# Four RWKV norm items moved between the output tiles of a hybrid encoder layer

## What is computed

```
h = rms_norm(x) ; u = h @ w_in                 # combined projection
y_a = rwkv7(u)   # 8 heads x 64, both directions; then per head a norm over 64,
                 #   y * lnx_w + lnx_b, + bonus, * g
y_b = hgrn2(u)   # 4 heads x 128, both directions; then per head
                 #   o * rsqrt(mean(o^2)) * gnorm_w, * silu(gate)
x = x + concat(y_a, y_b) @ w_out
h2 = rms_norm(x)
x = x + hierarchical_moe(h2)   # top-1 of 4 groups, top-2 of 8 experts in it, 32 experts
return rms_norm(x)
```

## Time and profile before

| | |
|---|---|
| median of 3 runs | 2428.27 us (2427.3 to 2428.68) |
| the profiled execution | 2425.25 us, span 2423.6 us |
| TensorE busy | 2266.9 us, 94% of the span |
| VectorE busy | 1028.8 us, 42% |
| ScalarE busy | 719.3 us, 30% |
| GpSimd busy | 418.3 us, 17% |
| DMA, mean | 180 GB/s, 436.48 MB |

### The profile page before, as it was taken

The page is one execution under the profiler, slowest core; times in us unless marked ns, Lnnn a source line. Parts: engine busy times, 40 slices in busy tenths (PEclk is TensorE's granted clock), DMA queues, the critical chain, the costliest instruction groups (busy, mean ns, idle before and its releaser), DMA issues. The chain is left out here.

```text
span 2423.6 us, 64805 instructions
## 1 busy us (share of the span) xinstructions
PE 2266.9 (94%) x28110; PEld 1485.1 (61%) x28110; DVE 1028.8 (42%) x2175; ACT 719.3 (30%) x1446; POOL 418.3 (17%) x520
## 2 busy tenths in 40 slices
PE   7989999989999999999968888995899999999997
PEld 4444544445555555555556656753788888888883
DVE  3236777634745645645645645543111111111115
ACT  4224554534544534534512312221000000000003
POOL 1002222200000000000012100012433334333331
PEclk9999999999999999999969988997899999999999
DMA  4113343533342432432366733251899999999986
GB/s 137 35 49 130 133 153 122 190 71 90 90 125 65 117 99 69 121 95 68 109 193 179 214 111 102 92 184 48 325 360 358 332 360 332 357 331 357 363 308 227
DMA packets 359836, 436.48 MB, mean 180 GB/s; under 512 B 164896, under 2 KB 296112, under 8 KB 351408
## 3 DMA queue, kind: packets, MB, share of 16 engines
q1 hardware_dynamic: 343232, 397.94, 48.2%
q0 software_dynamic: 14256, 35.04, 5.9%
q10 hardware_dynamic: 2112, 0.01, 0.1%
HBM read 329.87 MB, written 102.93 MB: 179 GB/s over the span
## 5 line engine op out<-in xcount | busy, mean ns | idle before, releaser
L1161 PE MATMUL h_pp<-hT,r_wcol 128*128 128x512 f32 x832 | 414.1, 621 | 9.1 <-ACT h_iraw L1289 9.1
L2715 PE MATMUL e_ps_gu<-e_xT,e_wg 128*128 128x128 f32 x2048 | 236.6, 277 | 18.3 <-DVE e_xT L2790 18.3
L2715 PEld LDWEIGHTS e_ps_gu<-e_xT,e_wg 128*128 128x128 f32 x2048 | 233.8, 194 | 18.8 <-DVE e_xT L2790 18.8
L2715 PEld LDWEIGHTS e_ps_gu<-e_xT,e_wu 128*128 128x128 f32 x2048 | 233.7, 192 | 14.8 <-issue 14.8
L2715 PE MATMUL e_ps_gu<-e_xT,e_wu 128*128 128x128 f32 x2048 | 233.9, 275 | 0.0
L2724 PE MATMUL e_ps_y<-e_wd,e_hid 128*128 128x512 f32 x512 | 225.1, 593 | 1.1 <-DVE e_hid L2804 1.1
L1161 PEld LDWEIGHTS h_pp<-hT,r_wcol 128*128 128x128 f32 x832 | 142.1, 190 | 130.2 <-issue 109.2
L500 PE MATMUL h_pp<-hT,r_wcol 128*128 128x512 f32 x480 | 209.0, 593 | 1.3 <-DVE hT L770 1.3
L2797 DVE TENSOR_SCALAR e_y<-e_ps_y,e_row 128x512 f32<-128x512 f32 x32 | 24.0, 750 | 336.0 <-PE e_ps_y L2724 336.0
L2724 PEld LDWEIGHTS e_ps_y<-e_wd,e_hid 128*128 128x128 f32 x512 | 95.0, 191 | 108.3 <-issue 108.3
L500 PEld LDWEIGHTS h_pp<-hT,r_wcol 128*128 128x128 f32 x480 | 90.3, 190 | 109.7 <-issue 108.0
(11 more groups left out here) (374 smaller groups left out, 3456.8 us busy)
## 6 DMA issues: line engine op xcount, KB each, us to landing
e_wg<-in_moe_w_gate_dram SPq DMA_DIRECT2D x32, 2048.0 KB
e_wu<-in_moe_w_up_dram SPq DMA_DIRECT2D x32, 2048.0 KB, 14.6
e_wd<-in_moe_w_down_dram SPq DMA_DIRECT2D x32, 2048.0 KB
r_wcol<-in_w_in_dram SPq DMA_DIRECT2D x35, 512.0 KB, 5.3
ar<-r_ar SPq DMA_DIRECT2D x24, 512.0 KB, 2.7
kb<-r_kb SPq DMA_DIRECT2D x24, 512.0 KB, 2.8
m_ar<-ar SPq DMA_DIRECT2D x48, 256.0 KB, 4.7
m_kb<-kb SPq DMA_DIRECT2D x48, 256.0 KB, 3.5
```

What stands on the lines that cost most here:

```text
L1161: last = nc.tensor.matmul(pp[n % 2][:], wcol[(k + 2) % 3][:, c], self.hT[:, c, span(s)], start=c == 0, stop=c == KT - 1)
L2715: last = nc.tensor.matmul(ps[:, q * P:(q + 1) * P], w[u][:, c, q * P:(q + 1) * P], xT[u][:, c * P:(c + 1) * P], start=c == 0, stop=c == KT ...
```

## The change

The list and the order of the units are rewritten. The units of the norm (`SEQ`) are now eight RWKV items, then HGRN tile 0, and from there RWKV item 8, HGRN 1, item 9, HGRN 2, item 10, HGRN 3, item 11, and the other HGRN tiles. The first eight RWKV items stay in front with the `r_half` of six tiles. The last four are entries (`more`) in the blocks of the output tiles n = 0 to 3. Within a block the squares of an HGRN tile come one block earlier (`norm("n_sq", n + 2)`), and for the six early tiles `half(n, 0)` stands before the turning of the rows of tile n - 1; for these tiles it was behind the first turn. Entries of output tiles carry their own due times. A gap no longer stops at an entry that is not due: it takes the first entry of the list that is. Rings and semaphore counts follow the new order of the units, and SP loads the last four blocks of `w_out` with items 4 to 7, the slots with item 6 and the router's parameters with item 7.

```diff
-        UNITS = ITEMS + TILES
+        LEAD = 8
+        SEQ = [("r", k) for k in range(LEAD)] + [("h", 0)]
+        for n in range(1, TILES):
+            SEQ += [("r", LEAD + n - 1)] * (LEAD + n - 1 < ITEMS) + [("h", n)]
+        UNITS = len(SEQ)
...
+                def more(name, k, cost=0.0):
+                    if LEAD <= k < ITEMS:
+                        out.append((name, (at["r", k] if name[0] == "n" or name == "r_gate" else k,), cost, ready(k - LEAD)))
 
                 def late(name, n, cost, *more):
                     if 0 <= n < TILES:
-                        out.append((name, (n,) + more, cost, 0))
+                        out.append((name, (n,) + more, cost, ready(n)))
 
                 def route(name, n, *more):
                     g = (n - 1) // 2 - 1
                     if n % 2 and 0 <= g < LAST_PAIR:
-                        out.append((name, (g,) + more, 0.4 if name == "rank" else 0, 0))
+                        out.append((name, (g,) + more, 0.4 if name == "rank" else 0, ready(2 * g + 1)))
...
                 norm("n_sq", 0)
                 norm("n_ss", 0, 0.9)
+                more("n_sq", LEAD)
                 norm("n_inv", 0)
+                more("n_ss", LEAD)
                 norm("n_wide", 0, 1.1)
+                norm("n_sq", 1)
                 for n in range(TILES + 1):
-                    norm("n_sq", n + 1)
+                    k = LEAD + n
+                    more("r_sum", k + 1)
+                    more("r_next", k)
+                    more("n_inv", k)
                     late("h2n", n - 1, 0)
-                    if n >= EARLY:
-                        late("half", n, 3.5, 0, 0)
+                    late("half", n, 3.5, 0, int(n < EARLY))
                     norm("n_ss", n + 1, 0.9)
                     route("choose", n, 0)
                     late("turn", n - 1, 1.1, 0)
                     if n == TILES:
                         route("place", n - 1)
                     norm("n_inv", n + 1)
-                    late("half", n, 3.5, 0, 1)
+                    late("half", n, 3.5, int(n < EARLY), 1)
+                    more("n_wide", k, 1.1)
+                    more("n_sq", k + 1)
                     norm("n_wide", n + 1, 1.1)
+                    norm("n_sq", n + 2)
                     route("choose", n, 1)
                     if n >= EARLY:
                         late("half", n, 3.5, 1, 0)
                     route("choose", n, 2)
                     if n < TILES - 1:
                         route("weigh", n)
+                    more("r_gate", k)
                     late("turn", n - 1, 1.1, 1)
-                    late("half", n, 3.5, 1, 1)
+                    if n >= EARLY:
+                        late("half", n, 3.5, 1, 1)
+                    more("n_ss", k + 1)
                     late("x1", n, 0)
                     late("routed", n - 1, 1.7)
                     route("rank", n)
...
                 def gap(c, budget):
-                    while rest and budget > 0 and rest[0][3] <= c:
-                        name, args, cost, _ = rest.pop(0)
+                    while budget > 0 and any(item[3] <= c for item in rest):
+                        name, args, cost, _ = rest.pop(next(i for i, item in enumerate(rest) if item[3] <= c))
                         run(name, *args)
                         budget -= cost
...
-                        elif k < PAIRS + RING_X:
+                        if PAIRS <= k < PAIRS + RING_X:
                             load_x(k - PAIRS)
-                        elif k == KY:
+                        if PAIRS <= k < KY:
+                            load_wout(k)
+                        if k == KY - 2:
...
-                        elif k == KY + 1:
+                        if k == KY - 1:
...
-                        if k >= ITEMS - PAIRS:
-                            load_wout(k - ITEMS + KY)
```

More of the change, by code:

```diff
@@ L1760, in goes_to, with g_full @@
                 return t, t < mirror(t) if d else t > mirror(t)
+            def g_full(p):
+                return g_loaded[p % RING_G], sum(32 if is_r(q) else 16 for q in range(p % RING_G, p + 1, RING_G))
             def summed(t):
@@ L1775, in fillers, with lead, early @@
                 out = []
[L1776 to L1791, removed]
-                ready = lambda n: max(FINISHED[n], mirror(FINISHED[n])) if n < TILES else 0
+                at = {item: p for p, item in enumerate(SEQ)}
+                ready = lambda n: max(FINISHED[n], mirror(FINISHED[n])) if n < TILES else 0
+                def lead(name, k, cost=0.0):
+                    if 0 <= k < LEAD + (name == "r_sum"):
+                        out.append((name, (k,), cost, -1))
+                def early(name, n, cost, *more):
+                    if 0 <= n < EARLY:
+                        out.append((name, (n,) + more, cost, -1))
                 def norm(name, n, cost=0.0):
                     if n < TILES:
-                        out.append((name, (ITEMS + n,), cost, ready(n)))
+                        out.append((name, (at["h", n],), cost, ready(n)))
+                def more(name, k, cost=0.0):
+                    if LEAD <= k < ITEMS:
+                        out.append((name, (at["r", k] if name[0] == "n" or name == "r_gate" else k,), cost, ready(k - LEAD)))
                 def late(name, n, cost, *more):
                     if 0 <= n < TILES:
-                        out.append((name, (n,) + more, cost, 0))
+                        out.append((name, (n,) + more, cost, ready(n)))
                 def route(name, n, *more):
@@ L1870, in schedule @@
                     if TILES_P <= c < TILES_P + 2:
-                        while ("x1", (2 * (c - TILES_P) + 1,), 0, 0) in rest:
+                        while any(item[:2] == ("x1", (2 * (c - TILES_P) + 1,)) for item in rest):
                             name, args, _, _ = rest.pop(0)
@@ L1959, in load_y, with load_g @@
                         sp.dma_start(ob[u][:], rows[1]).then_inc(y_loaded[u], 16)
-                    def load_g(k):
-                        if k >= UNITS:
+                    def load_g(p):
+                        if p >= UNITS:
                             return
[L1964 to L1974, removed]
+                        u, back, t = p % RING_G, p - RING_G, FINISHED[num(p)]
+                        if back >= 0:
+                            self.waits(sp, (dve_r if is_r(back) else dve_h).at("gated", num(back)))
+                        for dst, src_of in ((bv, self.bonusv), (gt, self.rgate)) if is_r(p) else ((gt, self.hgate),):
+                            sp.dma_start(by_k(dst[u][:]), src_of[:, :, tile(t)].rearrange("j p t -> p j t")
                                          ).then_inc(g_loaded[u], 16)
@@ L2117, in n_wide @@
                     def n_wide(k):
-                        self.waits(eng, dve_norm.at("odd", k) if is_r(k) else act_wide.at("wide", k - ITEMS),
+                        self.waits(eng, dve_norm.at("odd", num(k)) if is_r(k) else act_wide.at("wide", num(k)),
                                    bank_x.free(("wide", k)))
@@ L2197, in n_ss @@
                         r = var[k % 2][:, 0:2 * PAIRS if is_r(k) else PAIRS]
-                        self.waits(eng, dve_var.at("var", k) if is_r(k) else bank_y.done(("ss", k)))
+                        self.waits(eng, dve_var.at("var", num(k)) if is_r(k) else bank_y.done(("ss", k)))
                         nc.scalar.activation(r, r, ACT.Sqrt).then_inc(*act_root.inc("root"))
@@ L2323, in n_ss @@
                         r = var[k % 2]
+                        if k >= 2 and not is_r(k - 2):
+                            self.waits(eng, act_wide.at("wide", num(k - 2)))
                         if is_r(k):
@@ L2331, in n_ss @@
                         else:
-                            self.waits(eng, bank_y.full(("ss", k)), act_wide.ago("wide", k - ITEMS, 2))
+                            self.waits(eng, bank_y.full(("ss", k)))
                             nc.vector.tensor_scalar(r[:, 0:PAIRS], ps_y[:, 0:PAIRS], 1.0 / P, EPS_H, ALU.mult, ALU.add
```

52 lines of the change are left out of this document (36 added, 16 removed).

## The result

The changed kernel takes 2490.19 us (median of 4, 2484.4 to 2494.67) against 2427.78 us before: a ratio of 1.0255 (95% interval 1.0241 to 1.0269), 62 us slower. The direction was forecast, the size was not: +33.8 us was predicted, and the time lies above the range of 2436 to 2480.

The account below looks back on a forecast made before the run. TensorE, busy 94% of the span, was taken as the bound, losing time to waits and a lowered clock. Idle +24.7 and clock +9.1 us gave +33.8: 2425.25 to 2459.1, with 3.0 for the median 2462; range 2436 to 2480.

Parts of the forecast that it names:

- A: End of c = 4: ss and wide of the first HGRN item wait, VectorE still busy; 6.1 us idle.
- B: c = 5 after kv: wide of HGRN 1 waits for the bank, half(1,0) for x1(0); 6.5 us idle.
- E: c = 6: waits for the bank of item 10, routed, and half(3,0) behind x1(2); 3.8 us idle.
- F: End of c = 6: waits for the bank of item 11, then ss and wide of HGRN 4; 6.2 us idle.
- G: c = 7: routed(3) waits 0.65 us, routed(4) 4.6 us for ScalarE's copy queued behind weigh; 5.3 us idle.
- I: c = 9: turn(7,0) waits for h2, routed(7) follows, rank(3) waits for choose; 11.6 us idle.
- J: c = 10: waits for the state update, then HGRN 8's square, chain and gate; 5.1 us idle.
- K: c = 11: half(9,0) waits for x1(8), then HGRN 10's chain and the bank; 3.9 us idle.
- the clock: TensorE slowed behind waits: 29.4 us lost after the change against 20.3 before, +9.1 us.
- (d): Rival: the clock also costs 1.8 us after each of seven uncharged short waits, +12.6 us, 2475; 0.13 with the loads rival.
- (e): Rival: the loads SP issues earlier cost their bound, +7.5 us on top, 2470; chance 0.13 with the clock-after-every-cluster rival.
- (b): Rival: faster, as VectorE answers in time everywhere in c = 5 to 9; -19 us, 2410; chance 0.14.

Follow-up runs that it names:

- second profile: The changed kernel, unaltered, measured and profiled once more on another occasion: 2481.86 us, ratio 1.0212.
- Experiment 6: Changed kernel with 48 idle matmuls on TensorE in the places where it waits, order kept: 2447.67 us, ratio 1.0092.
- Experiment 7: Changed kernel with idle matmuls only in five long waits (28): 2473.16 us, ratio 1.0179; only in twelve short waits (20): 2472.08 us, ratio 1.0176.
- experiment 1: Changed kernel with only the old gap rule back, stopping at an entry that is not due: 2445.88 us, ratio 1.0066.
- experiment 2: Kernel before with only the new gap rule and due times: 2491.5 us, ratio 1.0253.
- experiment 8: Changed kernel with ScalarE's weigh behind its copy of the turned rows, and choose, rank and place due one pair later: 2471.92 us, ratio 1.0188.
- experiment 3: Changed kernel with all twelve RWKV items in front again: 2468.09 us, ratio 1.0164; with the old gap rule back as well: 2444.13 us, ratio 1.0075.
- experiment 4: Changed kernel with the halves of the six early tiles back where they stood, behind the first turn: 2502.06 us, ratio 1.0299.
- experiment 5: Kernel before with one entry moved, the squares of the next HGRN tile ahead of x1: 2430.55 us, ratio 1.0018.
- experiment 9: Kernel before with idle matmuls in its own waits of the stage and ahead of the first scores: 2415.24 us, ratio 0.9947.

## Why the prediction was right in its places and wrong in its size

**The waits were right, place by place.** Idle us of TensorE, forecast and measured in the changed kernel:

| place | forecast | measured |
|---|---|---|
| A ss, wide of HGRN 0 | 0.75, 5.3 | 0.61, 7.29 |
| B bank, half(1,0) for x1(0) | 1.55, 4.9 | 1.69, 4.98 |
| C bank, routed | 1.5, 0.6 | 1.68, 0.69 |
| D chain, gate | 1.4, 1.6 | 1.44, 1.62 |
| E bank, routed, x1(2) | 1.5, 0.65, 1.6 | 1.69, 0.69, 1.54 |
| F bank, square, chain | 1.5, 2.35, 2.3 | 1.69, 1.69, 2.23 |
| G routed(3), routed(4) | 0.65, 4.6 | 0.69, 4.38 |
| H chain, gate | 1.6, 1.2 | 1.44, 0.87 |
| I turn(7), routed(7), rank(3) | 4.4, 0.65, 0.65, 5.9 | 2.98, 0.78, 0.69, 6.04 |
| J state, square, chain, gate | 1.2, 0.7, 1.6, 1.6 | 1.21, 0.61, 1.44, 1.61 |
| K x1(8), chain, bank | 1.4, 1.6, 0.9 | 1.41, 1.44, 0.93 |
| sum | 56.4 | 56.1, and 3.2 of others |

Their causes stand in the trace as predicted. VectorE at place B, all of it between wide of HGRN 1 (1406.75) and half(1,0) (1412.36): the HGRN product and gate, the gate of item 8, the reduction of item 9, and only then x1(0):

```profile
1407.42 0.75 DVE L2391 SCALAR_TENSOR_TENSOR y<-y,o_gn,o_ps_x 128x512 f32<-128x512 f32 x1 [1.63 <-PE o_ps_x L2150]
1408.20 0.69 DVE L2395 TENSOR_TENSOR y<-y,o_gt 128x512 f32<-128x512 f32 x1
1408.81 0.69 DVE L2383 TENSOR_TENSOR y<-y,o_bv 128x512 f32<-128x512 f32 x1
1409.53 0.69 DVE L2385 TENSOR_TENSOR y<-y,o_gt 128x512 f32<-128x512 f32 x1
1410.14 0.68 DVE L2358 TENSOR_REDUCE o_var<-o_sq 128x8 f32<-128x512 f32 x1
1410.85 0.17 DVE L2361 TENSOR_SCALAR o_var<-o_var 128x8 f32<-128x8 f32 x1
1410.93 0.69 DVE L2401 TENSOR_TENSOR y<-o_ps_out,y 128x512 f32<-128x512 f32 x1
1411.54 0.68 DVE L2402 TENSOR_TENSOR y<-o_ps_out,y 128x512 f32<-128x512 f32 x1
```

The other two long ones on TensorE, for ScalarE's copy and for choose, and the last row of the stage, the half that ends at 1719.1 and not at some 1693:

```profile
1530.86 1.49 PE L2186 MATMUL o_ps_y<-o_wr,o_h2T 128*128 128x36 f32 x6 [4.38 <-ACT o_h2T L2265]
```

```profile
1602.66 1.11 PE L2179 MATMUL o_ps_x<-ident,o_x 128*128 128x128 f32 x4 [2.98 <-DVE o_x L2418]
...
1620.78 0.66 PE L1606 MATMUL o_ps_y<-q_picked,q_strict 128*128 128x64 f32 x2 [6.04 <-DVE q_before L1590]
```

```profile
1715.49 3.60 PE L2170 MATMUL o_ps_out<-o_wout,y 128*128 128x512 f32 x8
1718.93 1.87 PE L2186 MATMUL o_ps_y<-o_wr,o_h2T 128*128 128x36 f32 x16
```

**The term that failed is the clock.** The prediction says "29.4 us, against 20.3: +9.1". Busy time says +29.2 us. The clock's part of each trace (see the result) says which side was off: 16.9 us before, so the 20.3 was 3 us too high, and 44.4 us in the changed kernel and 50.0 us in its second profile, so the 29.4 was 15 to 21 us too low. I had taken the price of a wait, 1.8 or 3.3 us, from waits in the kernel before, charged each cluster once, and charged nothing for single waits under 1.3 us. In the kernel before the granted clock was back at its upper level for the rest of the stretch by 1508 us; in the changed one it fell twelve times up to 1641 us. Experiment 6 shows that the waits are the cause: filled, they leave 7.7 of the 44.4 us. Experiment 7 shows that neither the long waits nor the short ones are the missing part alone: each group, filled by itself, gave back about what the prediction had charged it (14.3 against 15.6, 14.9 against 13.8). What was too small is the whole, and how the 15 to 21 us divide between the waits stays open.

Rival (d) charged 12.6 us more, 42.0 us in all, and that is near the 44.4 us of the first profile; with the 20.3 us for the kernel before it still gave only 21.7 of the 29.2 us. By the rule of the Trainium skill that stood beside the sum (TensorE: Matmul & The Clock Gate, A second HAM failure mode: psum-queue depth-cycling), many short idles between groups of matmuls make the clock swing. The trace agrees: twelve falls of the clock, with waits of 0.3 to 7.3 us between the groups. My single row at 1553.56 was read too widely: TensorE had worked for 49 us before it, from 1503.58 on, without a wait that the profile shows.

**The range failed with it.** Its top stood just over (d) and didn't take in (d) with the rest of the clock. The 28 us between 2462 and 2490.19 are 20.1 us of clock, 2.8 us of idle time, 2.5 us outside the stretch, and 2.8 us from the median's distance to the profiled execution.

**Small misses.** At A the chain was 2 us longer (below), and turn(7,0) waited 2.98 us and not 4.4. Some 2.7 us of waits named "issue" inside two runs of scores weren't forecast. The loads, rival (e), cost little: from the second scores to the third, where they are denser, the changed kernel takes 0.5 us longer (28.4 us, 1263.61 to 1292.03, against 28.0, 1261.18 to 1289.14), and in its second profile the stretch from the first scores to the fifth turn_k is no longer than before (48.1 against 48.6 us). (b) falls with B and I. The direction and the mechanism, passed-over fillings that strip later tiles of their cover, are confirmed by experiments 1 and 2; that the rule alone would cost as much as the whole change was not predicted, and neither was that the third part of the change helps under the new rule only.

## What to carry to other kernels

Filling a wait by running ahead spends the cover of the next one: keep independent work in hand for each dependent chain to come, and look for what is left beside the last chain when the list is drained early. Don't price the clock by waits taken one by one: here the twelve short waits, 19.5 us in all, cost 14.9 us more in slow matmuls, the five long ones, 25.7 us in all, 14.3 us, and all the waits of the stage, 59 to 62 us, cost 44 to 50 us. Where waits can't be removed, idle matmuls in them are a cheap test of the clock's part, and here a gain of 0.5%.

## What the runs showed of the hardware that was not expected

Behind place and its scatters, scores(8) of the changed kernel takes 8.2 us (1493.42 to 1501.66) and not 4.0, with short stops for which the profile has no releaser:

```profile
1494.71 0.21 PE L2104 MATMUL o_ps_s<-e_wg,g_k 128*32 128x32 f32 x1 [0.41 <-issue]
...
1495.43 0.23 PE L2102 MATMUL o_ps_s<-e_wg 128*32 128x32 f32 x2 [0.41 <-issue]
...
1496.19 0.27 PE L2102 MATMUL o_ps_s<-e_wg 128*32 128x32 f32 x5 [0.47 <-issue]
1496.92 0.19 PE L2102 MATMUL o_ps_s<-e_wg 128*32 128x32 f32 x1 [0.46 <-issue]
```

They are in the second profile of the changed kernel and in those of experiments 6 (one, 0.77 us), 7 and 8 too, and in none of before and of experiments 1 to 5 and 9. They don't sit in one place of the code, and the new order alone doesn't bring them, since experiment 4 has none. All four profiles that were taken on the chip of experiments 7 and 8 have them, and of the eight on the chip of the other experiments only one does, so the chip is as good an explanation as the order (the chip of the changed kernel's first profile is not on record). The four take 1.75 us together; of the rest of the 4.2 us, the clock's part is seen in the last 16 wide matmuls, 3.62 us (at 1498.23) and not 1.97. What they are was not tried.

At place A two of VectorE's four prep instructions took 1.76 and 2.28 us, where the same two instructions take 0.7 and 1.2 in nearly all other steps of this profile:

```profile
1374.53 1.76 DVE L2312 TENSOR_TENSOR e_wg<-e_wg,g_to 128x512 f32<-128x512 f32 x1
1376.21 2.28 DVE L2315 TENSOR_TENSOR e_wd<-e_wg,g_to 128x1024 f32<-128x1024 f32 x1
1378.41 1.21 DVE L2319 TENSOR_TENSOR e_wu<-e_wg,g_upto 128x1024 f32<-128x1024 f32 x1
```

They overlap GpSimd's additions of full tiles, which the new order places there:

```profile
1374.19 1.54 POOL L1971 TENSOR_TENSOR o_spare<-o_spare,o_x 128x512 f32<-128x512 f32 x1
1375.70 1.70 POOL L1965 TENSOR_TENSOR y<-y,o_ob 128x512 f32<-128x512 f32 x1
```

This is the 2 us by which A's chain was longer. In the fourteen profiles on record these two instructions are slow 33 times in this stage, and every time they overlap such an addition of GpSimd (once in the kernel before too, at 1301.65 us, 1.75 us long); of the 283 times without such an addition beside them none is slow. But 20 of the overlaps left them at their usual length. So the addition beside them is what the slow ones have in common; no run here moves it alone.
